# One undivided fp32 product per tile in the output projection of a DeepNorm decoder layer

## The reference

```python
merged = g_attn * jnp.einsum('bsc,cd->bsd', y_attn, w_proj_attn) \
    + g_pool * jnp.einsum('bsc,cd->bsd', y_pool, w_proj_pool)
out = jnp.einsum('bsd,de->bse', merged, w_out)          # 256x2048 by 2048x2048
return layer_norm(DEEPNORM_ALPHA * x + out, ln_gamma, ln_beta)
```

## Time and profile before

| | |
|---|---|
| median of 2 runs | 954.57 us (954.43 to 954.7) |
| profiled execution | 954.86 us, of which the traced span is 953.1 us |
| mean granted TensorE clock | 0.998 |
| PE busy | 941.0 us (99%) |
| DVE, ACT busy | 637.2 us (67%), 423.1 us (44%) |
| DMA | 178.30 MB, mean 187 GB/s |
| output projection | 854.58 us to about 944.5 us of the span |

### The profile page before, as it was taken

How to read it: one execution, slowest core, us unless ns; L and a number is a source line. 1 busy time by engine, 2 the same in 40 slices (tenths; PEclk the granted TensorE clock), 3 DMA queues, 4 the chain that set the end, 5 groups by cost and what they waited for, 6 DMA issues and landing times.

```text
span 953.1 us, 15031 instructions
## 1 busy us (share of the span) xinstructions
PE 941.0 (99%) x5388; PEld 836.5 (88%) x5388; DVE 637.2 (67%) x1001; ACT 423.1 (44%) x591; POOL 0.2 (0%) x4
## 2 busy tenths in 40 slices
PE   7999999999999999999999999999999999999996
PEld 6898898898898998998998999888888888888886
DVE  6767667667667567567567567666666666565866
ACT  6444344354354354354354354545445444443340
POOL 0000000000000000000000000000000000000000
PEclk9999999999999999999999999999999999999999
DMA  8845544544445544544544546655455554557432
GB/s 302 303 164 178 190 170 176 184 176 176 176 176 176 176 176 176 179 173 176 182 170 176 184 168 226 218 179 215 176 178 188 184 198 176 187 200 276 177 133 89
DMA packets 27688, 178.30 MB, mean 187 GB/s; under 512 B 3471, under 2 KB 4239, under 8 KB 7055
## 3 DMA queue, kind: packets, MB, share of 16 engines
q1 hardware_dynamic: 26928, 173.53, 50.4%
q10 hardware_dynamic: 740, 4.50, 1.2%
HBM read 175.92 MB, written 2.10 MB: 187 GB/s over the span
## 4 chain that ended last, share of the span: by engine, by line
PE 97%; DMA 1%; SPq 1%; DVE 1%; issue 0%; ACT 0%; DVEq 0%
PE proj_ps L345 40%; PE proj_ps L346 20%; PE attn_ps L345 6%; PE attn_ps L339 4%; PE attn_ps L341 4%; PE attn_ps L340 4%; PE attn_ps L346 3%; PE value_ps L339 3%; PE value_ps L341 3%; PE value_ps L340 3%; DMA w_raw<-in_weights 1%; PE mixed_ps L339 1%; PE mixed_ps L341 1%; PE mixed_ps L340 1%; PE mixed_ps L453 1%; PE attn_ps L414 1%
## 5 line engine op out<-in xcount | busy, mean ns | idle before, releaser
L345 PE MATMUL proj_ps<-xt,w_hi 128*128 128x512 f32 x1664 | 584.3, 396 | 3.1 <-DVE w_lo L767 1.8
L346 PE MATMUL proj_ps<-xt,w_lo 128*128 128x256 f32 x1664 | 463.5, 279 | 0.0
L738 DVE TENSOR_TENSOR w_lo<-w_raw,w_hi 128x1024 fp32r<-128x1024 f32 x316 | 371.5, 1219 | 76.6 <-ACT w_hi L583 75.2
L345 PEld LDWEIGHTS proj_ps<-xt,w_hi 128*128 128x128 f32 x1664 | 312.9, 188 | 77.9 <-DVE xt L760 2.5
L583 ACT ACTIVATE w_hi<-w_raw 128x1024 fp32r<-128x1024 f32 x316 | 316.3, 1051 | 49.9 <-PE mixed_ps L341 26.4
L346 PEld LDWEIGHTS proj_ps<-xt,w_lo 128*128 128x128 f32 x1664 | 313.6, 188 | 0.0
L602 ACT ACTIVATE corr<-proj_ps 128x256 f32<-128x256 f32 x104 | 40.0, 385 | 285.5 <-PE proj_ps L346 285.5
L752 DVE TENSOR_TENSOR qk_f<-proj_ps,corr 128x256 f32<-128x256 f32 x48 | 20.3, 423 | 74.7 <-ACT corr L602 74.7
L345 PE MATMUL attn_ps<-ya,w_hi 128*128 128x512 f32 x128 | 45.3, 393 | 0.0
L345 PE MATMUL attn_ps<-yp,w_hi 128*128 128x512 f32 x128 | 45.1, 392 | 0.0
L340 PE MATMUL attn_ps<-w_lo,xt 128*128 128x384 f32 x128 | 42.8, 335 | 0.0
(11 more groups left out here) (162 smaller groups left out, 905.1 us busy)
## 6 DMA issues: line engine op xcount, KB each, us to landing
w_raw<-in_weights SPq DMA_DIRECT2D x158, 1024.0 KB, 4.8
res<-in_x_rows ACTq DMA_DIRECT2D x1, 2048.0 KB
out_rows<-res SPq DMA_DIRECT2D x8, 256.0 KB, 2.2
xt_raw<-in_xt SPq DMA_DIRECT2D x3, 512.0 KB, 7.7
w_raw<-in_weights SPq DMA_DIRECT2D x6, 256.0 KB, 7.6
w_raw<-in_weights SPq DMA_DIRECT2D x2, 512.0 KB, 10.5
gamma<-in_gamma_row ACTq DMA_DIRECT2D x1, 1024.0 KB
beta<-in_beta_row ACTq DMA_DIRECT2D x1, 1024.0 KB
```

Of the source, the lines that this page charges most:

```text
L345: mm(bank, w_hi[:, slot, cols], tile.rearrange("p a s -> p (a s)"), start=first, stop=False)
L346: return mm(bank[:, SEQ:2 * SEQ], w_lo[:, slot, cols], tile[:, 0, :], start=False, stop=last)
L738: tt(w_lo[:, slot, cols], w_raw[:, slot, cols], w_hi[:, slot, cols].bitcast(F32), ALU.subtract).then_inc(lo_split, 1)
```

## The change

In the output projection each product is one matmul of undivided fp32: the stationary operand is `merged`, now one fp32 tile of 256 columns per input tile, and the moving operand is the raw chunk in `w_raw` itself. So ACT's copies and DVE's subtractions of the 14 chunks 147 to 160 are gone, and so is the split of each merged tile on DVE (L834, L835 and the separate sum), of which one addition into `merged` is left. PE waits for the arrival of a chunk instead of its split. A raw slot is now held until its chunk is multiplied, so SP's loads of chunks 148 to 159 wait for `chunk_done` of the chunk three before. Chunk 160 goes to `last_raw`, in the place of `last_hi`, as the first of these loads: it waits for the end of chunk 144. Chunks 145 and 146 are still split in the gate stage's loop, and nothing reads the parts.

```diff
--- before.py
+++ after.py
@@ -159,7 +159,7 @@
         _, (zeros,) = place(at_ya, [("zeros", [512], F32R)])
 
         end_b, (yp, merged) = place(at_phase, [
-            ("yp", [POOL_TILES, 2, SEQ], F32R), ("merged", [OT, 2, SEQ], F32R)])
+            ("yp", [POOL_TILES, 2, SEQ], F32R), ("merged", [OT, SEQ], F32)])
 
         _, (yp_f,) = place(end_b - 2 * 2 * SEQ * 4, [("yp_f", [2, 2 * SEQ], F32)])
 
@@ -170,8 +170,8 @@
             ("rows_hi", [D_MODEL], F32), ("rows_signed", [D_MODEL], F32)])
         _, (shift_rows, row_parts) = place(at_szp, [
             ("shift_rows", [TT, P], F32R), ("row_parts", [D_MODEL], F32R)])
-        _, (last_hi, last_lo, beta, shifted) = place(base, [
-            ("last_hi", [CHUNK], F32R), ("last_lo", [CHUNK], F32R), ("beta", [D_MODEL], F32),
+        _, (last_raw, beta, shifted) = place(base, [
+            ("last_raw", [CHUNK], F32), ("beta", [D_MODEL], F32),
             ("shifted", [2, BLOCK], F32)])
 
         _, (corr_pair, pair_f) = place(at_szp, [("corr_pair", [2, SEQ], F32), ("pair_f", [2, SEQ], F32)])
@@ -239,7 +239,8 @@
         yp_f_ready = sem("yp_f_ready")
         yp_hi_done = sem("yp_hi_done")
         yp_split = sem("yp_split")
-        merged_split = sem("merged_split")
+        merged_ready = sem("merged_ready")
+        last_landed = sem("last_landed")
         first_rows_done = sem("first_rows_done")
         last_rows_done = sem("last_rows_done")
         rows_added = sem("rows_added")
@@ -306,7 +307,7 @@
             for j in range(1, RING):
                 sp.wait_ge(lo_split, 2 * (j + 1))
                 load(j, RING + j)
-            whole = (CHUNKS - RING) // RING
+            whole = C_FIRST // RING
             with sp.Fori(1, whole) as i:
                 for j in range(RING):
 
@@ -314,8 +315,15 @@
                     sp.dma_start(w_raw[:, j, :],
                                  stream_d[bass.ds(i * RING + (RING + j), 1), :, :]
                                  .rearrange("a p n -> (a p) n")).then_inc(raw_landed[j], 16)
-            for n in range(RING * (whole + 1), CHUNKS):
+            for n in range(RING * (whole + 1), C_FIRST + RING):
                 sp.wait_ge(lo_split, 2 * (n - RING + 1))
+                load(n % RING, n)
+            sp.wait_ge(lo_split, 2 * (C_FIRST + AHEAD))
+            sp.wait_ge(chunk_done, FROM + C_FIRST)
+            sp.dma_start(last_raw[:, :], stream_d[CHUNKS - 1, :, :]).then_inc(last_landed, 16)
+            for n in range(C_FIRST + RING, CHUNKS - 1):
+
+                sp.wait_ge(chunk_done, FROM + n - RING + 1)
                 load(n % RING, n)
 
             for n in range(TT * BLOCKS):
@@ -515,49 +523,50 @@
                         chunk(B_FIRST, j, i, B_CHUNKS, from_y)
                     next_bank(B_FIRST, j, i)
 
-            def out_weights(n, part):
-                return (last_hi, last_lo)[part][:, :] if n == CHUNKS - 1 else (w_hi, w_lo)[part][:, n % RING, :]
-
-            def out_products(n, kk, t):
+            def out_chunk(n):
+
+                if n == CHUNKS - 1:
+                    pe.wait_ge(last_landed, 16)
+                    return last_raw[:, :]
+                pe.wait_ge(raw_landed[n % RING], 16 * (n // RING + 1))
+                return w_raw[:, n % RING, :]
+
+            def out_product(weights, n, kk, t):
 
                 c, k = (n - C_FIRST) // BLOCK_CHUNKS, (n - C_FIRST) % BLOCK_CHUNKS * BLOCK_KT + kk
                 cols, tokens = slice(kk * BLOCK, (kk + 1) * BLOCK), slice(t * P, (t + 1) * P)
                 if k == 0 and c >= 2:
 
                     pe.wait_ge(rows_added, TT * (c - 2) + t + 1)
-                return product(block_sum(c, t)[:, :], merged[:, k, 0, tokens], merged[:, k, 1, tokens],
-                               out_weights(n, 0)[:, cols], out_weights(n, 1)[:, cols], k == 0, k == KT - 1)
-
-
-            pe.wait_ge(merged_split, OT - 1)
+                return mm(block_sum(c, t)[:, :], merged[:, k, tokens], weights[:, cols],
+                          start=(k == 0), stop=(k == KT - 1))
+
+
+            pe.wait_ge(merged_ready, OT - 1)
 
             for n in range(C_FIRST, CHUNKS - BLOCK_CHUNKS):
                 if n == C_FIRST + BLOCK_CHUNKS - 1:
 
-                    pe.wait_ge(merged_split, OT)
+                    pe.wait_ge(merged_ready, OT)
+                weights = out_chunk(n)
                 for kk in range(BLOCK_KT):
-                    if kk % 2 == 0:
-
-                        pe.wait_ge(lo_split, 2 * n + kk // 2 + 1)
                     for t in range(TT):
-                        done = out_products(n, kk, t)
+                        done = out_product(weights, n, kk, t)
                 done.then_inc(chunk_done, 1)
 
             for n in range(CHUNKS - BLOCK_CHUNKS, CHUNKS):
+                weights = out_chunk(n)
                 for kk in range(BLOCK_KT):
-                    if kk % 2 == 0:
-
-                        pe.wait_ge(lo_split, 2 * n + kk // 2 + 1)
-                    done = out_products(n, kk, 0)
+                    done = out_product(weights, n, kk, 0)
             done.then_inc(first_rows_done, 1)
 
             for h in range(2):
                 pe.wait_ge(rows_added, (TT + 2, TT * 3)[h])
                 for k in range(KT):
-                    n, kk = CHUNKS - BLOCK_CHUNKS + k // BLOCK_KT, k % BLOCK_KT
-                    cols = slice(kk * BLOCK + h * HALF_BLOCK, kk * BLOCK + (h + 1) * HALF_BLOCK)
-                    done = product(last_sum(h), merged[:, k, 0, P:SEQ], merged[:, k, 1, P:SEQ],
-                                   out_weights(n, 0)[:, cols], out_weights(n, 1)[:, cols], k == 0, k == KT - 1)
+                    weights = out_chunk(CHUNKS - BLOCK_CHUNKS + k // BLOCK_KT)
+                    at = k % BLOCK_KT * BLOCK + h * HALF_BLOCK
+                    done = mm(last_sum(h), merged[:, k, P:SEQ], weights[:, at:at + HALF_BLOCK],
+                              start=(k == 0), stop=(k == KT - 1))
                 done.then_inc(last_rows_done, 1)
 
             pe.wait_ge(shift_ready, 1)
@@ -689,17 +698,6 @@
             act.dma_start(beta[:, :], beta_d).then_inc(tail_landed, 16)
             act.dma_start(rows[0:ROWS, :], rows_d).then_inc(tail_landed, 16)
             act.dma_start(row_kind[0:ROWS, 0:2], row_kind_d).then_inc(tail_landed, 16)
-            whole = (OT - AHEAD) // RING
-            with act.Fori(0, whole) as i:
-                for j in range(RING):
-                    split_hi(C_FIRST, j + AHEAD, i, RING)
-            for e in range(whole * RING + AHEAD, OT - 1):
-                split_hi(C_FIRST, e, 0, 0)
-            landed(act, CHUNKS - 1, 0, 0, 0)
-            for half in range(2):
-                cols = slice(half * HALF * P, (half + 1) * HALF * P)
-                activation(last_hi[:, cols], w_raw[:, (CHUNKS - 1) % RING, cols], ACT.Copy).then_inc(hi_split, 1)
-
             activation(rstd[:, 4:5], ident[:, 0:1], ACT.Sqrt)
             for t in range(TT):
 
@@ -915,7 +913,7 @@
                         tt(yp[:, 2 * b:2 * b + 2, 1, :], yp_f[:, b % 2, :].rearrange("p (m s) -> p m s", m=2),
                            yp[:, 2 * b:2 * b + 2, 0, :].bitcast(F32), ALU.subtract).then_inc(yp_split, 1)
 
-            per_b = 4 * 5
+            per_b = 4 * 3
             start_b = chain.count
             with dve.Fori(0, B_STEPS) as i:
                 chain.i, chain.per = i, per_b
@@ -934,8 +932,8 @@
                            ALU.add).then_inc(proj_free, 1)
                         freed(B_FIRST, j, i)
                         chain.link(tt(pair_f[:, :, :], pair_f[:, :, :], gate[:, :, :], ALU.mult))
-                        chain.link(tt(sum_f[:, :], pair_f[:, 0, :], pair_f[:, 1, :], ALU.add))
-                        split(sum_f[:, :], merged, i * 4 + j // 3, merged_split)
+                        tt(tile_of(merged, i * 4 + j // 3), pair_f[:, 0, :], pair_f[:, 1, :],
+                           ALU.add).then_inc(merged_ready, 1)
             assert chain.count - start_b == per_b, chain.count - start_b
             chain.count, chain.per = start_b + per_b * B_STEPS, 0
 
@@ -1010,14 +1008,6 @@
 
             chain.link(nc.vector.memset(shift_parts[:, :, :], 1.0))
             for e in range(OT - 1):
-                if e + AHEAD < OT - 1:
-                    split_lo(C_FIRST, e + AHEAD, 0, 0)
-                if e + AHEAD == OT - 1:
-                    for half in range(2):
-                        cols = slice(half * HALF * P, (half + 1) * HALF * P)
-                        dve.wait_ge(hi_split, 2 * (CHUNKS - 1) + half + 1)
-                        tt(last_lo[:, cols], w_raw[:, (CHUNKS - 1) % RING, cols], last_hi[:, cols].bitcast(F32),
-                           ALU.subtract).then_inc(lo_split, 1)
                 if e % BLOCK_CHUNKS == BLOCK_CHUNKS - 1:
                     c = e // BLOCK_CHUNKS
 
```

## The result

The changed kernel takes 975.01 us in the median (974.54 to 975.48) against 954.57: a ratio of 1.0214, with a 95% interval from 1.017 to 1.0258. It is slower by 20.4 us, and the forecast was 974.5. With two runs of each kernel the interval leaves open whether that is more than two per cent.

A forecast was written before the change was run, and what follows sets the result against it. PE, busy 941.0 of 953.1 us, was taken as the bound; 17.6 + 2.2 us of dearer products on 954.86 gave 974.7, stated as 974.5. Own range 973.5 to 979; with the fp32r pace, 973 to 986.

The forecast's parts named there:

- PE bounds the stage: Output projection: only PE's own stream or its waits can move the end; removing splits on ACT and DVE gains 0.
- Four passes for three: Each output projection product: four passes, 0.857 us for 512 columns and 0.430 for 256; +17.6 and +2.2 us.
- a product with one divided side: Transposes of undivided fp32: the identity needs no dividing, so two passes, 0.1083 us for 128 columns; full products cost twice that.
- the fp32r pace (984.5): Rival for output projection products: four passes at the fp32r matmuls' pace, +30.0 us, 984.5 us; chance 0.14.
- the 9%: Output projection's fp32r matmuls: some 9% slower than one column a cycle, 0.2333 against 0.2133 us; not expected in fp32.
- faster (921.5): Rival for each product: two cycles per column with both sides full, 0.428 us for 512 columns, 921.5 us; chance 0.08.
- fourfold (1086): Rival for each product: four times the transposes' price per column, 1.733 us for 512, +132 us; chance 0.04 including low clock.
- Loads of the stationary tile and of the chunks hidden: Output projection: both loads run beside PE's passes, cost 0; chunk 159, the narrow place, at worst 2.7 us.
- the rival of exposed loads (1029): Rival: two uncovered weight loads of 0.19 us beside each of 144 products, +54.7 us more, 1029 us; chance 0.04.
- The tail unchanged: Behind the last matmul: the tail keeps its 8.4 us, change 0.

The follow-up runs named there:

- e_splits_kept: The changed kernel with the splits of chunks 147 to 159 put back on ACT and DVE, nothing reading them; 975.25 us, ratio 1.0213.
- e_ident: The changed kernel with the nine transposes of the probabilities of each head issued as ordinary fp32 matmuls by the identity; 985.54 us, ratio 1.0325.
- e_widths: The changed kernel with 512-column products cut into pieces of 256, 128 and 64 columns in the first three blocks; 1005.21 us in one run.
- e_three_16: The kernel before, with all three matmuls for input tiles 8 to 15 in bf16 from the same two tiles, true terms left out; 951.37 us, one run.
- e_late_loads: The changed kernel with the loads of chunks 148 to 159 issued one chunk later; 976.8 us, ratio 1.0231.
- e_two_terms: The kernel before, leaving out the output projection's product of high rows by low weights, all splits still made; 937.19 us in one run.
- The four variants with the same stage: e_ident, e_widths, e_late_loads and e_splits_kept, which keep the change; 985.54, 1005.21, 976.8 and 975.25 us.

## Why the prediction was right, step by step

- **PE bounds the stage, so only its stream counts.** Right: busy in each window of the stage at clock 1.00, before and after, and e_splits_kept shows that the chunk splits taken off ACT and DVE were free. That the merged tiles' split was free is read from the trace alone: PE runs into the stage without a gap at 854.86.
- **Four passes for three.** Right in number: 0.8583 us for 512 columns against the 0.857 taken, 0.4318 for 256 against 0.430. That is two records, each 512 columns at two cycles of 2.4 GHz (0.4267 us) and 2.5 ns. The reason given for it was wrong. The forecast took the transposes for a product with one divided side; e_ident shows that a product by the identity costs as much as any at 128 columns, and e_widths that at this width the load could set the pace as well. Two lines of reasoning stood behind the number. That both sides have a high and a low part is consistent with the time, though no trace shows what a pass multiplies. That the transposes show the price of one divided side does not hold, and that twice their pace gave the right number is luck. The Trainium skill, "FP8 and Floating Point Precision", section "TensorE Precision Notes", states four passes, and the time in the trace after agrees: 0.8583 us is 4.02 times 512 cycles.
- **Not at the fp32r pace (984.5).** Right: the 9% did not carry over to fp32, and in e_three_16 they were gone from the bf16 matmuls when no fp32r stood beside them.
- **Not faster (921.5), not fourfold (1086).** The trace has 0.858 us and not 0.428 or 1.733. The Trainium skill, "TensorE: Matmul & The Clock Gate", section "Terms", calls the transpose mode four times faster for fp32; here it was 2.1 times at 128 columns (0.2233 against 0.1083 us), where both stand near the floor of e_widths.
- **Loads of the stationary tile and of the chunks hidden.** Right, so the rival of exposed loads (1029) is out. e_widths and e_late_loads give the margins: 0.216 us against 0.112 for the one, 6.6 to 6.9 against 4.8 us for the other.
- **The tail unchanged.** Off by 0.28 us, with a granted clock of 0.62 against 0.74. The four variants with the same stage end with PE's small matmuls as fast as before and with tails of 8.34 to 8.72 us, so this looks like the scatter of single executions, as do the 0.28 us at the start. That the total came within 0.5 us owes something to how small they were.

## What to carry to other kernels

One fp32 matmul in place of three fp32r ones is one instruction for three, but two records in the trace, and took 1.23 times as long (0.8583 against 0.700 us). Where PE bounds the stage that is a loss of 0.158 us for each 512 columns, whatever it frees elsewhere. It could pay where ACT or DVE bind and PE has that time to spare; no run here shows such a case. When a price is read from a special instruction such as a transpose, measure the ordinary one before the reason is believed, even if the number fits.

## What the runs showed of the hardware

- An ordinary fp32 matmul is recorded as two matmuls, each with a load of its own. Such a record takes 0.4292 us for 512 columns, 0.2159 for 256, and 0.112 us for 128 and for 64 alike.
- fp32r matmuls start 0.2333 us apart at 512 columns, bf16 ones 0.2154; one bf16 between two fp32r gains nothing (0.700 us for the three).
- At 128 columns a product by the identity costs as much as by other data (0.2233 us), a transpose half of it (0.1083 us).
- After PE had stood still from 877 us on in e_two_terms, the granted clock fell to the 1.2 GHz level at 880 and was back at 887.
